# Router on the residual sum, two experts by request first, 26 experts sorted on TensorE

## The reference

```python
xs = layer_norm(DEEPNORM_ALPHA * xs + g1 * y, ln1_g[l], ln1_b[l])      # y is the mixers' output
y = hierarchical_moe(modulate(xs, sh2, sc2), *moe_w)                   # modulate: layer norm, * (1 + scale) + shift
xs = layer_norm(DEEPNORM_ALPHA * xs + g2 * y, ln2_g[l], ln2_b[l])

def hierarchical_moe(h, rg_w, rg_b, re_w, re_b, w_gate, w_up, w_down):
    g_logits = (h @ rg_w + rg_b)                # 4 groups of 8 experts, the best group is taken
    e_logits = (h @ re_w + re_b)                # 32 experts, the best two of the group are taken
    ...                                         # combine: a token's weight for each of the 32 experts
    hid = silu(einsum('bsd,edf->bsef', h, w_gate)) * einsum('bsd,edf->bsef', h, w_up)
    hid = hid * combine[..., None]
    return einsum('bsef,efd->bsd', hid, w_down)
```

## Time and profile before

| what | value |
|---|---|
| median of 3 runs | 1045.0 us (1041.93 to 1045.13) |
| profiled execution, its own time | 1046.35 us |
| span of its instructions | 1044.2 us |
| PE, PE weight load, DVE, ACT, POOL busy | 84%, 56%, 29%, 17%, 3% of the span |
| mean DMA rate | 311 GB/s |

### The profile page before, as it was taken

The page is one execution under the profiler, slowest core; times in us unless marked ns, Lnnn a source line. Parts: engine busy times, 40 slices in busy tenths (PEclk is TensorE's granted clock), DMA queues, the critical chain, the costliest instruction groups (busy, mean ns, idle before and its releaser), DMA issues.

```text
span 1044.2 us, 13222 instructions
## 1 busy us (share of the span) xinstructions
PE 873.0 (84%) x5572; PEld 583.7 (56%) x5572; DVE 304.0 (29%) x674; ACT 177.0 (17%) x387; POOL 26.5 (3%) x50
## 2 busy tenths in 40 slices
PE   4999999998986985679859998999998699567883
PEld 1787757876862442244338886587886345224321
DVE  2111323222557120101161233232346712110105
ACT  2101323210122110001021033142002211100001
POOL 0200000000000000000010000000000000000000
PEclk9899999999979998879979999999999889878997
DMA  9946963586648999999998315676555799999992
GB/s 378 409 181 276 384 242 125 205 286 249 280 189 327 432 426 430 430 412 396 426 422 348 148 34 198 274 293 242 161 242 192 292 430 429 428 428 428 427 426 106
DMA packets 38518, 324.48 MB, mean 311 GB/s; under 512 B 4920, under 2 KB 5048, under 8 KB 9392
## 3 DMA queue, kind: packets, MB, share of 16 engines
q1 hardware_dynamic: 34816, 313.02, 73.0%
q0 software_dynamic: 3200, 9.09, 2.7%
q10 hardware_dynamic: 432, 1.40, 0.3%
HBM read 321.06 MB, written 2.42 MB: 310 GB/s over the span
## 4 chain that ended last, share of the span: by engine, by line
PE 67%; DMA 21%; DVE 6%; issue 3%; ACT 3%; SPq 1%; DVEq 0%; ACTq 0%
DMA expert_gate_up<-in_w_gu 18%; PE ps L853 13%; PE ps L735 10%; PE ps L761 7%; PE ps L1014 6%; PE ps L928 5%; PE ps L1000 5%; PE ps L664 3%; PE ps L685 3%; DMA dense<-in_w_ada 2%; PE ps L875 2%; PE ps L965 2%; PE ps L823 2%; PE ps L705 2%; PE ps L886 2%
## 5 line engine op out<-in xcount | busy, mean ns | idle before, releaser
L853 PE MATMUL ps<-expert_gate_up,gathered_even 128*32 128x512 f32 x640 | 98.2, 679 | 57.6 <-DMA expert_gate_up<-in_w_gu 55.6
L735 PE MATMUL ps<-hT,dense 128*128 128x256 f32 x512 | 115.9, 385 | 0.0
L735 PEld LDWEIGHTS ps<-hT,dense 128*128 128x128 f32 x512 | 97.4, 193 | 16.1 <-issue 2.8
L853 PEld LDWEIGHTS ps<-expert_gate_up,gathered_even 128*32 128x32 f32 x640 | 28.9, 123 | 125.0 <-issue 125.0
L853 PE MATMUL ps<-expert_gate_up,gathered_odd 128*32 128x512 f32 x512 | 81.0, 592 | 7.1 <-DMA expert_gate_up<-in_w_gu 5.2
L761 PE MATMUL ps<-dense,hT 128*128 128x256 f32 (+1 forms) x320 | 69.4, 381 | 1.7 <-ACT hT L1130 1.7
L664 PE MATMUL ps<-dense,cond 128*32 128x256 f32 x768 | 55.3, 418 | 15.8 <-ACT cond L1223 11.8
L875 PE MATMUL ps<-expert_down,hiddenT 128*32 128x512 f32 x576 | 65.5, 594 | 2.3 <-ACT hiddenT L1194 2.3
L761 PEld LDWEIGHTS ps<-dense,hT 128*128 128x128 f32 x320 | 60.7, 201 | 10.4 <-ACT hT L1130 2.5
L1591 DVE TENSOR_TENSOR hidden<-hidden,ps 128x256 f32<-128x256 f32 x18 | 7.6, 421 | 200.8 <-ACT hidden L1190 200.8
L1014 PE MATMUL ps<-dense,zT 128*128 128x256 f32 x256 | 57.9, 388 | 4.2 <-DMA dense<-in_w_out 2.9
(11 more groups left out here) (239 smaller groups left out, 1029.2 us busy)
## 6 DMA issues: line engine op xcount, KB each, us to landing
expert_gate_up<-in_w_gu SPq DMA_DIRECT2D x64, 2048.0 KB, 18.2
expert_down<-in_w_dn SPq DMA_DIRECT2D x64, 1024.0 KB, 20.4
dense<-in_w_ada SPq DMA_DIRECT2D x48, 1024.0 KB, 9.1
dense<-in_w_in SPq DMA_DIRECT2D x28, 1024.0 KB, 11.8
dense<-in_w_o SPq DMA_DIRECT2D x8, 1024.0 KB, 6.1
dense<-in_w_out SPq DMA_DIRECT2D x8, 1024.0 KB, 4.8
dense<-in_w_c SPq DMA_DIRECT2D x4, 1024.0 KB, 28.4
dense<-in_w_uq SPq DMA_DIRECT2D x4, 576.0 KB, 6.0
```

Source lines behind the costliest of these rows:

```text
L735: last = mm(b[:, m * 256:(m + 1) * 256], w[:, k, m * P:(m + 1) * P], hT[:, k, :], start=(k == 0), stop=(k == KD - 1))
L853: last = mm(ps[32 * j:32 * j + 32, bank, :], xg[n % 2][:, k, at_ + j * CAP:at_ + (j + 1) * CAP], w_gu[BUFFER[held[j]]][:, k, :], start=(k ...
```

## The change

- **Router on the residual sum.** Layer norm is affine in its input once its mean and deviation are known. GpSimd makes weights from the router's, the modulation and layer norm 1's gain and offset, centred over the features (`route_weights`, `centred_weights`: twelve tensor operations in each layer; TensorE sums over partitions in `sums`). TensorE transposes `t_res` (`turn_t`) and multiplies these; VectorE applies the two deviations afterwards (`half_logits`, `logits`).
- **First group by request.** Group 0 holds experts 0 and 1 alone, two tiles each, one for each request. Its tokens are gathered from `xh2`, before scale and shift, which ScalarE and VectorE apply when they copy them out. Group 1 holds experts 2 to 5. There are now 10 groups and 6 chunks. Six experts get double tiles.
- **Sorting.** Experts 6 to 31 are sorted with products on TensorE (`totals`, `order_experts`, `turn_route`, `sort_route`); none of their loads is issued before `order` is there.
- **Tokens as rows.** `h` is `xh2` times rows of scale plus rows of shift, on VectorE; GpSimd loads the two sets of rows (1 MB each) in the gap. There is no `turn_tokens` any more. Expert 5's down weights are loaded earlier.

The diff, cut to its core:

```diff
-FIXED = 2 * EPI
+FIXED = SLOTS
...
-GROUPS = 9
 SPLIT = 5
-FIRST_OF = (0, 4, 8, 10, 12, 16, 20, 24, 28)
...
+TILES = ((0, 1, 0, 1), (2, 3, 4, 5), (6, 6, 7, 7), (8, 8, 9, 9), (10, 10, 11, 11), (12, 13, 14, 15),
+         (16, 17, 18, 19), (20, 21, 22, 23), (24, 25, 26, 27), (28, 29, 30, 31))
+BY_REQUEST = 1
+CHUNKS = 6
...
+                TT(part[0], router, wide(cols[:, 3, :, :]), ALU.mult)
+                link(TT(part[1], router, wide(cols[:, 2, :, :]), ALU.mult))
+                over_features(0, 2 * third, third, third + third // 2)
+                b, n = nth(l, ("sums", 0))
+                pool.wait_ge(drained[b], n + 1)
+                link(TT(part[0], part[0], mean_, ALU.subtract))
+                TT(part[1], part[0], both(ln1c[:, 0, :]), ALU.mult)
+                link(TT(part[2], part[0], both(ln1c[:, 1, :]), ALU.mult))
+                over_features(third, 0, 2 * third, 2 * third + third // 2)
...
+                nc.gpsimd.tensor_tensor(part[0], part[1], mean_, ALU.subtract).then_inc(weights_ready, 1)
...
+                centred_weights(l)
+                pool.wait_ge(out_drained, 8 * (l + 1))
+                load_rows(pool, l, 4, scale2, rows2_in)
+                pool.wait_ge(x1_ready, 2 * l + 2)
+                b, n = nth(l, ("route", 1))
+                pool.wait_ge(filled[b], n + 1)
+                load_rows(pool, l, 3, shift2, rows2_in)
...
+            def gather_first(w, s):
+
                 for c in range(2):
...
+                    for k in range(4 * c, 4 * c + 4):
+                        at_ = k % 4 * OWN
+                        last = mm(ps[:, FIRST_BANK[s][c], at_:at_ + OWN], xh2[:, s, k * P:(k + 1) * P],
+                                  sel[:, 0, s, 0:OWN].bitcast(F32), start=True, stop=True)
+                    last.then_inc(w["xg_filled"], 1)
...
+                totals(l)
+                gathered(m, 0)
+                evacuated(l, ("route", 1), ("count", 0), ("count", 1))
+                gate_up(m, None, 0, 0, ks=range(0, 4))
+                order_experts(l)
+                gate_up(m, None, 0, 0, ks=range(4, KD))
+                turn_group(m, 0, 0, 0)
+                pe.wait_ge(*reached(m, "sel_ready", 3))
+                pe.wait_ge(lo_ready, 2 * (l + 1))
+                gather(m, 1, (1, 2, 3, 1))
+                gathered(m, 1)
+                down(m, None, 0, 0)
+                gate_up(m, None, 1, 1)
...
+                select_T(m, 0, 0)
+                turn_route(l)
...
+                turn_group(m, 1, 1, 1)
+                sort_route(l)
...
+                select_T(m, 1, 1)
...
+                scatter(m, 0, 0, True)
+                pe.wait_ge(*reached(m, "sel_ready", 4))
+                gather(m, 2, (0, 2, 3, 0))
+                gathered(m, 2)
+                select_T(m, 2, 0)
+                down(m, None, 1, 1)
...
+            def half_logits(l, s):
...
+                V.scalar_tensor_tensor(lg[:, s, :, :].rearrange("p g e -> p (g e)"), b[:, 0:RW], rstd[:, 4 + s:5 + s],
+                                       offset1[:, s, :], ALU.mult, ALU.add).then_inc(gone, 1)
...
+            def tokens(l, s):
+
+                dve.wait_ge(xh2_ready, 2 * l + s + 1)
+                dve.wait_ge(rows2_in, 32 * (l + 1))
+                link(V.tensor_tensor(h[:, s, :], xh2[:, s, :], scale2[:, s, :], ALU.mult))
+                V.tensor_tensor(h[:, s, :], h[:, s, :], shift2[:, s, :], ALU.add).then_inc(h_ready, 1)
```

More of the change, by code:

```diff
@@ L813, in gather, with totals @@
-            def gather(w, n, banks, evacs):
-                cols = CHUNK if n < CHUNKS - 1 else CHUNK // 2
+            def totals(l):
+                pe.wait_ge(ada_biased, 8 if l == 0 else 12)
+                for h in range(2):
+                    for s in range(2):
+                        last = mm(ps[32 * h:32 * h + 32, ADA_BANK, 0:8], member[:, s, :], const[:, C_ONES:C_ONES + 8],
+                                  start=(s == 0), stop=(s == 1), skip_group_check=True)
+                last.then_inc(sort_filled, 1)
@@ new lines, in gather_own @@
+            def gather_own(w, s):
+                for c in range(2):
+                    for k in range(4 * c, 4 * c + 4):
+                        at_ = k % 4 * OWN
+                        for hp, part in enumerate((h_hi, h_lo)):
+                            last = mm(ps[:, 2 * s + c, at_:at_ + OWN], part[:, s, k * P:(k + 1) * P], sel[:, 0, s, 0:OWN],
+                                      start=(k % 4 == 0 and hp == 0), stop=True, skip_group_check=True)
+                    last.then_inc(w["xg_filled"], 1)
@@ L1344, in bias_ada @@
                 g = part % ADA
-                rows = len([p for p in range(part) if p % ADA not in COLUMN_PARTS])
+                rows = len([p for p in range(part) if p % ADA in ROW_PARTS])
                 if g == 0:
@@ new lines, in low_tokens, with gathered_first @@
+            def low_tokens(l, s):
+                dve.wait_ge(hi_ready, 2 * l + s + 1)
+                V.tensor_tensor(h_lo[:, s, :], h[:, s, :], h_hi[:, s, :].bitcast(F32), ALU.subtract).then_inc(lo_ready, 1)
+            def gathered_first(w):
+                dve.wait_ge(*reached(w, "xg_filled", 4))
+                for k in range(4, KD):
+                    at_ = k % 4 * OWN
+                    last = V.tensor_scalar(xg_own[:, k, OWN:2 * OWN], ps[:, FIRST_BANK[1][1], at_:at_ + OWN],
+                                           cols[:, 3, 1, k:k + 1], cols[:, 2, 1, k:k + 1], ALU.mult, ALU.add)
+                last.then_inc(w["xg_dve"], 1)
@@ L1762, in _ @@
                 dve.wait_ge(post1_in, 48 * (l + 1))
-                for i in range(4):
-                    output(l, 0, i)
+                output(l, 0, 0)
+                output(l, 0, 1)
+                route_offsets(l)
+                output(l, 0, 2)
+                output(l, 0, 3)
                 e = mean(0, 4, 4, LN_EPS)
```

789 lines of the change are left out of this document (472 added, 317 removed).

## The result

The changed kernel takes 1050.6 us (median of 14 runs, 1046.9 to 1053.1) against 1045.1 for the kernel before (14 runs). The ratio is 1.0057, with a 95% interval of 1.0039 to 1.0074. By the medians it is slower by 5.6 us, where 3 us of gain were forecast. The profiled execution has a span of 1049.0 us against 1044.2.

What follows compares the result with a forecast made beforehand. Expert parts were taken as bound by loads, each layer's end by its last load's landing. Layer changes of −1.3 and −1.7 gave −3.0 on 1046.35, so 1043.3; the median lies 1.35 lower: 1042, range 1033 to 1052.

Steps and rivals of the forecast that it cites:

- D moves by +3.1: D, the end of the output projection, comes 3.1 us later from added TensorE work, at 292.1 and 792.55.
- S = D+13.8: S, the start of the first `gate_up`, comes 13.8 us after the output projection's end, at 305.9 and 806.35.
- `gate_up` 0 ends at S+7.2: Group 0's `gate_up` on TensorE ends 7.2 us after its start: 7.0 with two small products.
- rival 2: Clock falls in short pieces between output projection and first `gate_up`: about 5 us a layer, 1047 to 1052; chance 0.18.
- VectorE has the number chain until S+4.4: Behind the first `gate_up`'s start, VectorE is busy with the number chain for 4.4 us, then makes the split tokens.
- I charge 3 us: Low clock behind TensorE's pause after group 0's `gate_up` costs 3 us, between 0 and 7, before group 1 ends.
- the release: End of group 1's `gate_up`, freeing buffers for the next four experts; forecast at S+31.8.
- 168.7 us to the last landing: From group 1's `gate_up` end to the last expert's gate and up weights landing: 1.5 + 34 × 4.88 + 1.3.
- Layer 0 waits another 4.4 us: Loading expert 22 must wait for TensorE's `gate_up` 6: 4.4 us more in layer 0, none in layer 1.
- At a fixed distance: Each layer's end follows the last weight landing at a fixed distance, since what follows is not changed.
- rival 3: GpSimd is late, so TensorE stands before `sums`; at 8 ns an element 5 and 7 us, 1054; chance 0.10.
- Rival 4: TensorE's work in ten groups becomes the bound: 3 us more in groups 1 to 6 gives 1048; chance 0.15.

Runs made afterwards that it cites:

- gap_filled: Changed kernel plus 18 identity transposes in TensorE's short waits between the output projection and the first `gate_up`; 1041.2 us, 0.9970 of the kernel before.
- tokens_first: Changed kernel with VectorE making the split tokens ahead of the sorting, second low part ahead of group 0's product; 1031.3 us, 0.9867 of the kernel before.
- no_rows: Changed kernel without the two row loads, tokens made from `x` instead (other output); 1050.4 us, 1.0053 of the kernel before.
- pause_filled: Changed kernel plus 36 identity transposes in TensorE's pause behind group 0's `gate_up`; 1041.8 us, 0.9971 of the kernel before.
- both_filled: Changed kernel plus 18 transposes ahead of the first `gate_up` and 36 in the pause behind it; 1039.7 us, 0.9949 of the kernel before.
- before_filled: Kernel before plus 32 identity transposes in TensorE's wait for the second half of the normalised tokens; 1038.2 us, 0.9951 of the kernel before.

## Why the prediction was wrong, point by point

- *"D moves by +3.1"*: held, 2.95 us in both layers (255.81 to 289.4 against 258.30 to 288.96). The terms as listed add up to 3.3.
- Two readings were off without harm: the terms from D to S add up to 13.6 and not 13.8, and the slices 14 to 22 hold 348 to 432 GB/s, not 412 to 432.
- *"S = D+13.8"*: D+15.4 and D+14.4. The second gather ran at half clock for the most part in layer 0 (3.39 us for 2.0) and for a small part in layer 1 (2.32). With the clock held S is at D+14.1: the step's sum was right to 0.3 us, the clock in it was not.
- *"`gate_up` 0 ends at S+7.2"*: **this failed.** 10.3 and 9.8 us. It is the mechanism of rival 2, which I put at 0.18 because the longest idle piece would be short. It was (0.99 us), and the clock fell anyway. gap_filled shows it: with the pieces filled, 7.4 us. Rival 2's total, "about 5 us in a layer", came near: undoing it gave 9.4 us of the kernel. Its place did not, so that is partly luck: rival 2 put the cost on the pieces between D and S, which lost 1.4 and 0.3 us, while `gate_up` 0 behind S lost 3.1 and 2.6.
- *"VectorE has the number chain until S+4.4"*: S+7.1 and S+6.5. I priced the products of the chain with a `gate_up` at full clock around them; with the clock held in gap_filled the tokens begin at S+4.2. The low parts came at S+16.4 and S+15.8 instead of S+14.1. I had also taken the order of VectorE's list as given. That is no miss of the forecast, which had the same order in it; but tokens_first shows that turning it round is worth 19 us, where each filling gave 9.
- *"I charge 3 us"* for the clock behind the pause, between 0 and 7: **mis-sized.** Gather (7.06 for 3.5) and `down` (6.46 for 3.64, 6.17 in layer 1) took 6.4 and 6.1 us more. The advice against idle gaps that the prediction quotes from the Trainium skill (TensorE: Matmul & The Clock Gate, Why this matters for your kernels) was right in sign, and the size was twice what I gave it.
- Together the release was due at D+45.6 and came at D+52.9 and D+50.9, 7.3 and 5.3 us late. Of these 1.6 and 0.6 lie ahead of S, 2.3 and 1.7 between S and the low part, and 3.4 and 3.1 behind it. In each of the three the granted clock was at 0.50 for a part of the time, where the forecast had full clock or, behind the pause, 3 us for it. By the earlier trace rows and the measured 171.1 us behind it, break-even with the kernel before was near D+50 in layer 0 and D+46 in layer 1.
- *"168.7 us to the last landing"*: 171.1 in both layers (342.3 to 513.4, 844.3 to 1015.4), 1.4 more than with the 1 us of leftovers. *"Layer 0 waits another 4.4 us"* for expert 22: it did not. `gate_up` 6 ended 97.0 us behind the release (forecast 102.0), and the loads ahead of expert 22 need 99.1. So layer 0 was spared 3 us, which hid part of the miss. *"At a fixed distance"*: from the last landing to the start of the last `down` it was 10.0 and 11.7 us before and 10.5 and 10.6 in the changed kernel, so layer 1 got 1.1 us back there that the forecast did not count. The lead of 2.5 us from the start of the program is luck as well: without it the last landing in layer 0 would be some 2.5 us later.
- *GpSimd hidden* (rival 3): held. The first five operations took 5.8 us, as these rows show (timeline of GpSimd, changed kernel):

```profile
219.50 1.27 POOL L650 TENSOR_TENSOR route_weights<-router_w,ada_columns 128x640 f32<-128x640 f32 x1
220.73 1.26 POOL L651 TENSOR_TENSOR route_weights<-router_w,ada_columns 128x640 f32<-128x640 f32 x1
222.07 1.61 POOL L633 TENSOR_TENSOR route_weights<-route_weights 128x640 f32<-128x640 f32 x1
223.76 0.87 POOL L635 TENSOR_TENSOR route_weights<-route_weights 128x320 f32<-128x320 f32 x1
224.71 0.59 POOL L636 TENSOR_TENSOR route_weights<-route_weights 128x160 f32<-128x160 f32 x1
```

  They ended 7 us before TensorE's sums. The Trainium skill (GPSIMD Engine Reference, Performance versus the Vector engine) gave an estimate of 5.3 us. The 6 us that it has for the first call to a freshly loaded kernel (Instruction dispatch) do not show here, the first of the five took 1.27 us.
- *The rows beside the loads*: held, no_rows measured the same time. *Rival 4* (ten groups): 2 us at most, and only once the release is much earlier.

That the release sets the end was argued from the trace in the prediction; the table shows it. That the clock ahead of S, the clock behind the pause and VectorE's order each delay the release, and by how much, is shown by gap_filled, pause_filled and tokens_first. How the time divides between clock and order can't be told exactly, since the two overlap: a longer `gate_up` delays the tokens, and late tokens make the pause that lowers the clock. The two kernels with fillings, both_filled at 1039.7 and before_filled at 1038.2, are the same within their intervals: with such fillings in both, though they hold the clock in neither throughout, the change as written shows no gain. Of the variants here it pays clearly only with VectorE's list in the other order.

## What to carry to other kernels

When a change opens a shorter path, list what each engine waits for in its new place: here an engine with 5.8 us of idle time waited for two tiny products in the middle of another engine's long group, with independent work standing behind the wait. Price a stretch with many short waits at TensorE's half clock as well, and see which side of break-even that lands on. Filling the waits with cheap transposes is a quick test of this, and in the kernel before it was worth 6 us. Read the clock behind the filling too, since it can fall there instead.

## What was not expected of the hardware

- Behind a stretch with no pause longer than 0.99 us the granted clock fell to 0.50 (1.2 GHz), in both layers of the changed kernel. 18 transposes in these pauses, 2 us of work, kept it at 1.00 (2.4 GHz) up to the end of `gate_up` 0, in both layers of gap_filled.
- In both_filled the clock held through three short waits (0.86, 0.79 and 0.56 us) behind the second filling in layer 1, and fell behind the first two of them in layer 0. In before_filled it held through the stretch behind the filling and fell before the first `gate_up` began, in both layers.
